# One denominator product per head: GpSimd adds up the blocks of weighed scores in the mLSTM cells of a two-block kernel

## What is computed

```python
def step(carry, xs):
    ...
    s = jnp.einsum("bhtk,bhsk->bhts", qc, kc) * w_intra
    num = (jnp.einsum("bhts,bhsv->bhtv", s, vc)
           + w_inter[..., None] * jnp.einsum("bhtk,bhkv->bhtv", qc, c_st))
    den = jnp.sum(s, axis=-1) + w_inter * jnp.einsum("bhtk,bhk->bht", qc, n_st)
    h = num / jnp.maximum(jnp.abs(den), jnp.exp(-m_t))[..., None]
```

## Time and profile before

| | us |
|---|---|
| median of 3 runs | 2105.43 (2105.28 to 2106.63) |
| the profiled execution, its own time | 2098.56 |
| its span in the trace | 2096.8 |
| PE busy in the span | 1996.2 |
| POOL busy in the span | 362.4 |
| cells of layer 0 (transposes before open 0, to projection 6) | 1418.4 to 1489.5 |
| cells of layer 1 | 1861.3 to 1934.2 |

### The profile page before, as it was taken

The page is one execution under the profiler, slowest core; times in us unless marked ns, Lnnn a source line. Parts: engine busy times, 40 slices in busy tenths (PEclk is TensorE's granted clock), DMA queues, the critical chain, the costliest instruction groups (busy, mean ns, idle before and its releaser), DMA issues.

```text
span 2096.8 us, 21907 instructions
## 1 busy us (share of the span) xinstructions
PE 1996.2 (95%) x8662; PEld 1526.7 (73%) x8662; DVE 1228.6 (59%) x1636; ACT 844.0 (40%) x1264; POOL 362.4 (17%) x319
## 2 busy tenths in 40 slices
PE   7999999988977899999999999999999899999997
PEld 5888888756533478888887777776788778766886
DVE  5764444677696446665665686924662559335742
ACT  5331323201456543322333347644542366445531
POOL 2000001156244010000001302601201024102002
PEclk9999999998778999999999999999999999999998
DMA  5332232221000134654652222321123222220221
GB/s 185 100 118 75 100 104 97 84 71 53 26 0 1 65 131 158 208 182 158 198 173 68 71 91 78 101 81 51 51 91 100 83 86 81 91 70 31 91 90 61
DMA packets 53174, 196.70 MB, mean 94 GB/s; under 512 B 5969, under 2 KB 6481, under 8 KB 52433
## 3 DMA queue, kind: packets, MB, share of 16 engines
q1 hardware_dynamic: 42912, 159.50, 22.7%
q0 software_dynamic: 7504, 28.58, 4.3%
q10 hardware_dynamic: 2656, 7.23, 1.0%
HBM read 192.14 MB, written 2.10 MB: 93 GB/s over the span
## 4 chain that ended last, share of the span: by engine, by line
PE 78%; DVE 13%; ACT 4%; POOL 2%; issue 1%; DMA 1%; ACTq 0%; POOLq 0%; DVEq 0%
PE PS L554 77%; DVE AR L1546 3%; DVE AR L1779 2%; DVE WLO L1543 2%; ACT WHI L1078 1%; DVE AR L2021 1%; DVE AR L1869 1%; PE PS L768 1%; DVE AR L1988 0%; DMA H<-in_xT 0%; POOL ACC L2137 0%; DVE ACC L1546 0%; DMA RAW<-in_w_out 0%; ACT SQ L1093 0%; DVE AR L1759 0%
## 5 line engine op out<-in xcount | busy, mean ns | idle before, releaser
L554 PE MATMUL PS<-HNH,WHI 128*128 128x512 f32 x1632 | 658.7, 404 | 15.8 <-ACT HNH L1109 13.9
L1543 DVE TENSOR_TENSOR WLO<-RAW,WHI 128x1024 fp32r<-128x1024 f32 (+1 forms) x270 | 371.6, 1379 | 514.7 <-ACT WHI L1078 514.5
L554 PE MATMUL PS<-HNH,WLO 128*128 128x512 f32 x1632 | 639.8, 392 | 3.4 <-DVE WLO L1543 3.4
L1078 ACT ACTIVATE WHI<-RAW 128x1024 fp32r<-128x1024 f32 (+1 forms) x270 | 295.9, 1096 | 687.0 <-PE PS L554 613.3
L554 PE MATMUL PS<-HNL,WHI 128*128 128x512 f32 x1632 | 436.0, 390 | 0.1
L554 PEld LDWEIGHTS PS<-HNH,WHI 128*128 128x128 f32 x1632 | 308.2, 189 | 96.4 <-issue 22.0
L554 PEld LDWEIGHTS PS<-HNH,WLO 128*128 128x128 f32 x1632 | 308.5, 189 | 77.9 <-issue 8.9
L554 PEld LDWEIGHTS PS<-HNL,WHI 128*128 128x128 f32 x1632 | 307.4, 188 | 64.8 <-DVE HNL L1546 1.0
L554 PE MATMUL PS<-AR 128*128 128x512 f32 (+12 forms) x700 | 213.3, 519 | 8.7 <-DVE SQ L1763 3.6
L2137 POOL TENSOR_TENSOR ACC<-ACC,SQ 128x512 f32<-128x512 f32 x46 | 62.7, 1362 | 782.2 <-ACT SQ L1093 781.3
L554 PEld LDWEIGHTS PS<-AR 128*128 128x128 f32 (+5 forms) x700 | 99.4, 199 | 90.2 <-issue 57.6
(11 more groups left out here) (299 smaller groups left out, 2421.6 us busy)
## 6 DMA issues: line engine op xcount, KB each, us to landing
RAW<-in_w_in SPq DMA_DIRECT2D x80, 512.0 KB, 3.5
AR<-in_w_ada POOLq DMA_DIRECT2D x48, 512.0 KB, 3.9
RAW<-in_w13a SPq DMA_DIRECT2D x44, 512.0 KB, 3.3
RAW<-in_w13b SPq DMA_DIRECT2D x44, 512.0 KB, 4.2
RAW<-in_w_out SPq DMA_DIRECT2D x40, 512.0 KB, 3.5
RAW<-in_w2a SPq DMA_DIRECT2D x16, 704.0 KB, 4.1
RAW<-in_w2b SPq DMA_DIRECT2D x16, 704.0 KB, 5.6
RAW<-in_w_inA SPq DMA_DIRECT2D x12, 512.0 KB, 3.3
```

The lines of the kernel that those rows point to most:

```text
L554: return pe.matmul(o, l, r, start=start, stop=stop, skip_group_check=True)
L1078: act.activation(hi_of(name, i), raw_of(name, i), ACT.Copy).then_inc(*HI.up(name, i))
L1543: dve.tensor_tensor(lo_of(name, i), raw_of(name, i), f32(hi_of(name, i)), S_).then_inc(*LO.up(name, i))
```

## The change

The products with ones in `sums` go (four per head, 512, 384, 256 and 128 columns). The block j = 0 of weighed scores is now written into a full-width buffer of its own, `SUM` (two of them, by head), and POOL adds the blocks j = 1, 2, 3 into it as they come. At `finish`, one product of 512 columns with ones makes the denominator, in a bank that is taken there. ACT's magnitude now waits for that product (`den`). DVE waits for POOL's additions (`summed`) before it writes a score buffer anew.

```diff
-        SBF = [XR[:, 6, :], XR[:, 7, :]]
+        SUM = [XR[:, 3, :], ACC]
+        SBF = [XR[:, 6, :], XR[:, 7, :], XR[:, 6, :]]
+
+        def weighed(h, j):
+
+            return SUM[h % 2] if j == 0 else SBF[j - 1]
+
...
                         if j == 0:
-                            bd[h] = [take(pe, "cell_out", l, h, z) for z in range(3)]
+                            bd[h] = [take(pe, "cell_out", l, h, 1 + z) for z in range(2)]
...
-                        x = SBF[j % 2][:, P * j:T]
-                        mm(bd[h][0][0][:, P * j:T], ONES, x, j == 0, j == 3)
+                        x = weighed(h, j)[:, P * j:T]
                         pe.wait_ge(*A.at("v2", l, j, h // 2))
-                        mm(bd[h][1][0][:, P * j:T], V2[:, j, 256 * h:256 * h + P], x, j == 0, j == 3)
-                        mm(bd[h][2][0][:, P * j:T], V2[:, j, 256 * h + P:256 * h + 256], x, j == 0, j == 3).then_inc(*P_.up("sums", l, h, j))
+                        mm(bd[h][0][0][:, P * j:T], V2[:, j, 256 * h:256 * h + P], x, j == 0, j == 3)
+                        mm(bd[h][1][0][:, P * j:T], V2[:, j, 256 * h + P:256 * h + 256], x, j == 0, j == 3).then_inc(*P_.up("sums", l, h, j))
                     elif step == "finish":
-                        give(bd[h][0][1], A, "ab", l, h)
-                        give(bd[h][1][1], V, "cell", l, h, 0)
-                        give(bd[h][2][1], V, "cell", l, h, 1)
+                        ps, b = take(pe, "cell_out", l, h, 0)
+                        pe.wait_ge(*G.at("summed", l, h, 3))
+                        mm(ps[:, :], ONES, SUM[h % 2], True, True).then_inc(*P_.up("den", l, h))
+                        give(b, A, "ab", l, h)
+                        give(bd[h][0][1], V, "cell", l, h, 0)
+                        give(bd[h][1][1], V, "cell", l, h, 1)
...
-                        act.wait_ge(*P_.at("sums", l, h, 3))
+                        act.wait_ge(*P_.at("den", l, h))
...
-                        if j > 1:
-                            dve.wait_ge(*P_.at("sums", l, h, j - 2))
-                        elif h:
-                            dve.wait_ge(*P_.at("sums", l, h - 1, 2 + j))
+                        if j == 0 and h > 1:
+                            dve.wait_ge(*P_.at("den", l, h - 2))
+                        elif j == 3:
+                            dve.wait_ge(*P_.at("sums", l, h, 1))
+                            dve.wait_ge(*G.at("summed", l, h, 1))
+                        elif j and h:
+                            dve.wait_ge(*P_.at("sums", l, h - 1, 4 - j))
+                            dve.wait_ge(*G.at("summed", l, h - 1, 4 - j))
...
+                    elif step == "sums" and j[0]:
+                        j, = j
+                        s = SUM[h % 2][:, P * j:T]
+                        pool.wait_ge(*V.at("score", l, h, j))
+                        pool.wait_ge(*P_.at("sums", l, h, 0))
+                        mine()
+                        pool.tensor_tensor(s, s, weighed(h, j)[:, P * j:T], A_).then_inc(*G.up("summed", l, h, j))
```

More of the change, by code:

```diff
@@ L2067, in dve_program @@
                         dve.wait_ge(*A.at("weights", l, h, j))
-                        if j > 1:
-                            dve.wait_ge(*P_.at("sums", l, h, j - 2))
-                        elif h:
-                            dve.wait_ge(*P_.at("sums", l, h - 1, 2 + j))
-                        stt(SBF[q][:, P * j:T], bank("score", l, h, j)[:, P * j:T], 1.0 / 16, WB[q][:, P * j:T], M_, M_).then_inc(*V.up("score", l, h, j))
+                        if j == 0 and h > 1:
[6 more added lines that the diff above has]
+                            dve.wait_ge(*G.at("summed", l, h - 1, 4 - j))
+                        stt(weighed(h, j)[:, P * j:T], bank("score", l, h, j)[:, P * j:T], 1.0 / 16, WB[q][:, P * j:T], M_, M_).then_inc(*V.up("score", l, h, j))
                     elif step == "out_gate":
```

## The result

| | before | after |
|---|---|---|
| median of 20 runs each, us | 2101.77 (2099.02 to 2106.63) | 2108.74 (2104.11 to 2118.49) |
| the profiled execution, own time | 2098.56 | 2112.11 |

The ratio is 1.0038, 95% interval [1.0028, 1.0049], or 8.0 us slower (the medians lie 7.0 us apart; 8.0 goes by the ratio). The forecast was 8.6 us slower. As a time it was 2114.0 us, 5.3 us above what was measured: 3.7 us of that is the kernel before, whose median over 20 runs is 2101.77 us where the first three gave 2105.43.

What follows compares the result with a forecast made beforehand. PE was 95% busy, but in heads 1 to 3 ACT's chain was taken to set the time to block 2. Path terms of +1.8 us and clock falls of +6.8 us on 2105.43 gave 2114.0 us, range 2105.0 to 2121.0.

Steps and rivals of the forecast that it cites:

- the clock's 6.8 us: One fall of PE's clock at each of the four waits of heads 2 and 3, 1.69 us each, 6.8 us.
- Head 0 wins 2.16 us: Head 0 has no projection ahead and is PE bound, so all 2.16 us of removed ones products are won.
- Blocks 0 and 1 of heads 1 to 3 win nothing: 1.51 us removed per head lie under ACT's chain; PE waits 2.35 us in heads 2 and 3, about 1.5 in head 1.
- ACT's detour: From the projection's end to block 2, the chain over ACT, POOL and DVE that PE waits for, 6.81 us.
- Block 2 wins nothing, block 3 wins 0.22, the denominator costs 0.86: Block 3's 0.22 us is won three times a layer; the product at finish costs 0.86 us four times a layer.
- The last denominator waits 0.3 us, and the sum without the clock is +0.9 us per layer: PE waits some 0.3 us for POOL's last sum; path terms total +0.9 us per layer, +1.8 us for two.
- Additions of 0.95, 0.63 and 0.32 us: POOL's additions of 384, 256 and 128 columns, taken in proportion to 1.26 us at 512 columns.
- rival 3: POOL's addition holds block 3's select, 0.4 us in six heads, giving 2109.7 us; chance 0.06 as the main cause.
- POOL keeps its pace beside DVE's products of a PSUM and an SBUF operand: POOL's 384-column addition takes 0.95 us beside DVE, not the bound of 1.71, which would add 2.4 us.
- By the idle-gap rule the forecast would have been +1.8 us: A rule of thumb by which waits this short leave PE's clock up, so no clock term: +1.8 us.

Runs made afterwards that it cites:

- Experiment 3: The kernel before without the ones products of blocks 0 and 1 in heads 1 to 3: ratio 1.0003 to the kernel before.
- experiment 7: Changed kernel with ACT, DVE and POOL doing out_gate and gated at the head's end, and the projection's bank given back behind score 3: ratio 0.9924.
- 8: The kernel before with each head's two opening products fed from 128 rows instead of one: ratio 0.9969.
- 9: The changed kernel with each head's two opening products fed from 128 rows instead of one: ratio 1.0003 to the kernel before.
- experiment 1: The changed kernel without POOL's additions of blocks 1 to 3, the denominator's product running on block 0 alone: ratio 1.0038 to the kernel before.
- 2: The changed kernel with a denominator product of 128 columns instead of 512: ratio 1.0066 to the kernel before.
- experiment 4: The changed kernel with unread 512-column products added ahead of block 2, one in head 1, two in heads 2 and 3: ratio 1.0032.
- 10: The changed kernel with opening products fed from 128 rows and a denominator product of 128 columns instead of 512: ratio 0.9993.
- 6: The changed kernel with ACT, DVE and POOL doing out_gate and gated at the head's end: ratio 0.9973 to the kernel before.
- 12: The kernel of experiment 7 with projection 6 put ahead of the last denominator product: ratio 1.0003 to the kernel before.
- 5: The kernel before with ACT, DVE and POOL doing out_gate and gated at the head's end: ratio 0.9949.

## Why the prediction was right, and where it wasn't

The account of the paths held. That the total came out within 0.6 us (8.0 against 8.6) is in part luck: one term was 1.1 us too small, and the largest one, the clock's 6.8 us, was put at four places where the profile of the changed kernel has no fall.

- *Head 0 wins 2.16 us*: right. 10.99 - 8.83 = 2.16.
- *Blocks 0 and 1 of heads 1 to 3 win nothing*: right, and shown from both sides. Experiment 3 took 9.1 us of this work out for 1.0003; experiment 7, with ACT's detour out of the way, won 1.28 us per head. The projection's end to block 2 stayed 6.81 us. The waits are 2.34 us (2.35 forecast) and 1.30 in head 1 (about 1.5; the ends of products are modelled, so an idle time is known less well than a start).
- *Block 2 wins nothing, block 3 wins 0.22, the denominator costs 0.86*: right. Block 3 starts 1.48 us behind block 2. From opening 1 to opening 2, head 1's period, 18.59 us grew to 19.24, by 0.65 where 0.86 - 0.22 = 0.64 was forecast.
- *The last denominator waits 0.3 us, and the sum without the clock is +0.9 us per layer*: mis-sized. Falls taken out, layer 0 lost 90.50 - 1.69 - 87.57 = 1.24 us and layer 1 (92.46 - 3.25) - (89.28 - 1.69) = 1.6, together +2.9 us instead of +1.8. Experiments 8 and 9 give the same 2.9. The term that was too small is the last denominator's: the wait is 0.37 and 0.67 us, and with the slower start behind it it cost 0.66 and 0.96 us (experiment 1) where 0.3 was put in; -2.16 - 0.66 + 3.44 with these gives 1.28 and 1.58.
- *Additions of 0.95, 0.63 and 0.32 us*: a little longer, 0.99, 0.72 and 0.45, that is some 0.18 us each besides 0.21 us per 100 columns. They never held a select (rival 3): its spacing is 1.61 us, and without them (1) the waits ahead of block 2 stay as they are.
- *POOL keeps its pace beside DVE's products of a PSUM and an SBUF operand*: right, but not by the row that it was read from. In the earlier trace rows the addition of 1.26 us starts at 439.65, behind the end of DVE's product, 438.46 + 0.68 = 439.14, so it ran beside nothing. In the changed kernel the 384-column addition (1475.64) kept 1.00 us while DVE ran two such instructions, and none of the 24 took longer than 0.997 us. By this the trace agrees with the Trainium skill, GPSIMD Engine Reference, section 1 (Specifications).
- *The clock: a fall at each of the four waits of heads 2 and 3, 6.8 us*: for the profile of the changed kernel this is the step that failed, in its place and there in its size too. The cells' falls rose from 1.69 to 1.69 + 3.25 = 4.94 us, that is by 3.25 us, and they came behind head 1, at one-row openings, while all four waits of 2.34 us passed at full clock. The cause that was forecast is real, but not sure: with one-row openings, 9 of 16 such waits had a fall in four profiles (none of four in the changed kernel, two in 1, four in 2, three in 3); with full-row openings all four had one (9), and those four falls cost 4.7 us and not 6.8. What the forecast left out is the opening behind head 1, with its shorter wait: it had a fall in both layers of the changed kernel, 1, 2 and 4, and with full rows in neither layer of 9 and one of 10, which points to the one-row products as part of the cause. They don't bring a fall each time: experiment 3 has the same opening and wait and no fall there, and opening 0, with no wait ahead, has a fall behind it in layer 1 of before, 1, 6 and 12 and none in either layer of the changed kernel, 5 and 7. What decides between these places isn't shown.
- *By the idle-gap rule the forecast would have been +1.8 us*: the Trainium skill, TensorE: Matmul & The Clock Gate, section "HAM oscillation", has the clock fall for longer idle gaps than any in the cells. The runs disagree: four falls behind 2.34 us of waiting (9), and one in layer 1 of before in work without a wait.

What is still open: the cells of the one profile lost 6.1 us and the timing 8.0 us. With 2.9 us for the change itself, 5.1 us of the timed loss would be the clock's; the other runs may have had more falls, or falls in other places, but a profile exists only of one execution of each kernel. Nor is it settled why experiment 4, whose waits are short, is timed only 0.0006 below the changed kernel; its one fall per layer at the opening explains that it isn't at full clock, not that the four waits seem worth so little there.

## What to carry to other kernels

Before you count removed work as won, follow the chain that ends last on both sides of each removed instruction: here more than half of PE's saving lay beside ScalarE's detour of 6.81 us and turned into waiting, while the one product added lay on the path. Move the detour first; then the same change pays (1.0038 without the move, 0.9924 with it and with the PSUM bank given back later, against 0.9949 for the move alone, two intervals that overlap; in the cells, at full clock in both, it is 5.0 us). And price an added wait on TensorE twice, once as time and once as a chance that the clock falls in the work behind it, 0.5 to 1.7 us for a single fall in this kernel.

## What the runs showed of the hardware

- Less work on TensorE can lower its clock enough to lose more than was saved: 5.1 us of products less made the kernel 5.9 us slower, at a mean granted clock of 0.88 in the cells instead of 0.96 to 0.98 (2).
- A product with one row of weights and data isn't quicker than one with 128, and the clock fell at such products where it didn't at full ones. With 128 rows, the opening to the end of the scores took 4.72 us instead of 5.02, the two falls behind head 1 were gone (9), and the kernel before won 0.31% (8).
- A fall that lies partly over a wait costs less: 0.53 and 0.82 us in head 3, against 1.69 us in head 2, where PE was busy (9).
- Behind a wait the first product takes 0.11 us longer to its successor's start: 0.54 instead of 0.43 us for 256 columns and 0.33 instead of 0.22 for 128 (before, head 2, against 5).
- GpSimd's additions in SBUF have a fixed part: 0.45, 0.72 and 0.99 us for 128, 256 and 384 columns.
